# The last 512 columns of two projections in two pieces, and a first slot that multiplies high parts ahead of low parts

## The chip, the cores and the metric

The kernel runs on one core of one Trainium2 chip. The metric is the device time of one launch in microseconds (us), lower is better. TensorE does the matrix products, VectorE, ScalarE and GpSimd the rest, and SyncE issues most DMAs.

## What is computed

A decoder trunk of two layers on 256 tokens of width 1024, in float32. Cut to what matters here, a layer is

```python
x = layer_norm(alpha * x + (g_A * y_A + g_B * y_B) @ w_out, ln1_g, ln1_b)
x = layer_norm(alpha * x + (silu(conv(x @ w_up_gate)) * (x @ w_up_val)) @ w_down, ln2_g, ln2_b)
```

where y_A is a sparse attention and y_B a recurrent mix, both computed from x. The inner width of the second line is 2816. layer_norm takes the mean and the variance of the 1024 columns of each token, subtracts, scales by (var + eps)^-1/2 and applies a gain and a bias. There are four norms: A (after the out projection) and B (after the down projection) of layer 0 and of layer 1; the last one's result is the output.

## The kernel before, in words

**Split products.** The large products are float32 made of rounded parts: each weight block of 128 rows by 1024 columns lands in one of four ring slots, ScalarE copies its high part (split_hi, L1296 to L1303), VectorE subtracts to get the low part (splits_up_to, L1893 to L1902), and TensorE multiplies high by high, high by low and low by high (product, L737 to L742). Every engine runs its own list of instructions in the order in which it is written, and waits on semaphores where it needs another engine.

**Out and down projections** (token_major, L1197 to L1220). The result has the tokens on the partitions, two halves t of 128 tokens, and 1024 columns. It is held in four PSUM banks, 2 to 5, each one quarter (t, j): 128 tokens by 512 columns. For all weight blocks but the last four, each block does all four quarters. The last four blocks (the tail) are walked quarter by quarter: both quarters of t = 0, then quarter (1, 0), then quarter (1, 1). So the quarters become ready one after the other, the last with the last product. The out projection has 8 blocks, the down projection 22.

**The norm** (layer_norm, L1911 to L1992), on VectorE: added(k) adds quarter k to x in x_tok and takes its statistics with bn_stats; moments(t) merges them and adds epsilon; GpSimd raises to the power -1/2 (norm_rsqrt, L642 to L646); centered(t) subtracts the mean and multiplies by the gain; diagonal(t) makes a diagonal matrix of the scales. The written order is added 0, added 1, moments 0, centered 0, added 2, diagonal 0, added 3, moments 1, centered 1, diagonal 1. In the very last norm a first half of the output scaling ("n0a") stands in the place of diagonal 0, ahead of added 3, and no diagonal is made.

**Turning x.** TensorE multiplies x_tok by the diagonal (turned_half, L762 to L782), which scales and transposes: 16 products of 128 columns for each t, into four PSUM banks that x_banks names (L447 to L450): two pair banks (0 and 1), and 6 and 7. After norm A this is the turn "U": ScalarE evicts x's high part (xU_out, L1287), and VectorE then computes x's low part (L1980 to L1986), two column blocks at a time. After norm B of layer 0 it is the turn "T": the first products of layer 1 (L1055) stand between its two halves.

**Up projection** (split_blocks, L744 to L760). It has 22 pairs of slots, each slot 24 products of 256 columns. Slot ("up", 0) is the first. Its result goes into a pair bank, the same that holds the first two turned blocks, so every second block first waits until VectorE has made the low part of x and so has read that bank:

```python
parts = rhs(kb)
if n == ("up", 0) and b == 0 and kb % 2 == 0:
    pe.wait_ge(*dve_parts(l, f"x{kb // 2}"))
```

VectorE's order behind norm A is: diagonal 1, the low part of the first up slot's weights, the four low parts of x, the low part of the second slot's weights (L1978 to L1987), and then the rest. The slots' split high parts are made on ScalarE behind the wait for the slot that they replace.

Of the kernel before, what the change touches and what calls it, by code (L numbers as in the profile page):

```python
# [39 lines left out]
ALU = mybir.AluOpType  # L40
# [3 lines left out]
P = 128  # L44
D = 1024
T = 256
DEPTH = 2
TT = T // P
KB = D // P
# [158 lines left out]
def trunk(nc, x_in, pos_in, stream, lora_in, cpar_in, rpar_in, const_in, masks_in, out, x_dram, v_dram):  # L208
    ctx = ExitStack()
    with ctx:  # L210
        def sb(name, shape, dt=F32):
            return ctx.enter_context(nc.sbuf_tensor(name, shape, dt))
# [16 lines left out]
        def bank(n):  # L229
            return ps[:, n, :]  # L230
# [18 lines left out]
        def tok(n):  # L249

            return ps[:, n, :].rearrange("p (b t) -> p b t", t=T)
# [3 lines left out]
        x_tok = sb_or_parts("x_tok", [P, TT, D])  # L255
# [29 lines left out]
        ang = sb("ang", [P, 3, TT, NFR])  # L285
        pos = sb("pos", [P, TT], I32)
        posf = sb("posf", [P, TT])
        ln = sb("ln", [P, TT, 24])

        rs_ks, vs_dC = sb_or_parts("rs_ks", [P, 2, GB, T]), sb_or_parts("vs_dC", [P, 2, GB, T])  # L290
        tha_kkn, X_Y = sb_or_parts("tha_kkn", [P, 2, GB, T]), sb_or_parts("X_Y", [P, 2, NU, CH])
# [114 lines left out]
        slot_used = sem("slot_used")  # L406
# [14 lines left out]
        def used(l, kind, i):  # L421

            return slot_used, SLOT_AT[l, kind, i] + 1
# [21 lines left out]
        pair_at = {n: d for d, n in enumerate(pairs)}  # L445

        def x_banks(l, w):  # L447

            d = pair_at[l, ("up", 0)] if w == "U" else 0
            return d % 2, (d + 1) % 2, 6, 7  # L450

        def pair_done(l, n):
            return used(l, *pair_slots(n)[-1])
# [13 lines left out]
        def by_layer(name, steps):  # L467
            return Steps(sem(name), [steps] * DEPTH)
# [15 lines left out]
        def mids_by(gap):  # L484

            return sum(n <= gap for n in mid_last) + NM

        pe_x = by_layer("pe_x", [f"T{t}{i}" for t in range(TT) for i in range(4)] + [f"A{k}" for k in range(3)]
                        + [f"U{i}" for i in range(4)] + [f"B{k}" for k in range(3)])
        act_x = by_layer("act_x", [f"T0{i}" for i in range(4)] + ["T10", "T12"] + ["Aax"] + [f"U{i}" for i in range(4)] + ["Bax"])  # L490
        dve_par = by_layer("dve_par", ["dpar", "lsig"])
        def norm_steps(l, w):
            if l == DEPTH - 1 and w == "B":
                return ["add0", "st0", "add1", "st1", "mv0", "eps0", "c0", "add2", "st2", "n0a", "add3", "st3", "mv1", "eps1",
                        "c1", "n0", "n1a", "n1b"]
            return ["add0", "st0", "add1", "st1", "mv0", "eps0", "c0", "add2", "st2", "dg0", "add3", "st3", "mv1", "eps1",
                    "c1", "dg1", "n0", "n1a", "n1b"]

        dve_x = Steps(sem("dve_x"), [[f"mix{i}" for i in range(4)] + [w + n for w in "AB" for n in norm_steps(l, w)]
# [187 lines left out]
        def _(pe):  # L687
# [55 lines left out]

            def split_blocks(l, n, rhs):  # L744

                d = pair_at[l, n]

                def block(b, name):
                    if b == 0:
                        pe.wait_ge(*pair_free(*pairs[d - 2]))  # L750
                    w = slot_parts(l, *name)
                    for kb in range(KB):
                        parts = rhs(kb)
                        if n == ("up", 0) and b == 0 and kb % 2 == 0:
                            pe.wait_ge(*dve_parts(l, f"x{kb // 2}"))
                        mm = product(tok(d % 2)[:, b, :], [x[:, kb * P:kb * P + P] for x in w], parts,
                                     kb == 0, kb == KB - 1)
                    mm.then_inc(slot_used, 1)

                return [lambda b=b, name=name: block(b, name) for b, name in enumerate(pair_slots(n))]  # L760

            def turned_half(l, w, t):  # L762

                banks = x_banks(l, w)
                if w == "U":
                    pe.wait_ge(*dve_x(l, f"Adg{t}"))
                elif l:
                    pe.wait_ge(*dve_x(l - 1, f"Bdg{t}"))
                else:
                    pe.wait_ge(x_in_sbuf[t], 16 * (2 - t))  # L770
                for i in range(4):
                    for b in range(2):
                        dst = tok(banks[i])[:, b, t * P:t * P + P]
                        src = x_tok[:, t, (2 * i + b) * P:(2 * i + b + 1) * P]
                        if w == "T" and l == 0:
                            mm = pe.transpose(dst, src, ident)
                        else:
                            mm = pe.matmul(dst, src, diag[t], start=True, stop=True)  # L778
                    if w == "T":
                        mm.then_inc(*pe_x.inc(l, f"T{t}{i}"))  # L780
                    elif t:
                        mm.then_inc(*pe_x.inc(l, f"U{i}"))  # L782
# [261 lines left out]
            for l in L2:  # L1044
# [151 lines left out]

                def token_major(kind, n, lhs, wait, w_norm):  # L1197

                    def quarter(i, t, j):
                        w = slot_parts(l, kind, i)  # L1200
                        wait(i)
                        return product(bank(2 + 2 * t + j), [x[:, t * P:t * P + P] for x in lhs(i)],
                                       [x[:, j * 512:j * 512 + 512] for x in w], i == 0, i == n - 1)

                    tail = range(n - NS, n)
                    for i in range(n - NS):
                        for t in range(TT):
                            for j in range(2):
                                mm = quarter(i, t, j)
                        mm.then_inc(slot_used, 1)  # L1210
                    for i in tail:
                        for j in range(2):
                            mm = quarter(i, 0, j)
                            if i == n - 1:
                                mm.then_inc(*pe_x.inc(l, f"{w_norm}{j}"))
                    for i in tail:
                        mm = quarter(i, 1, 0)
                    mm.then_inc(*pe_x.inc(l, f"{w_norm}2"))
                    for i in tail:
                        quarter(i, 1, 1).then_inc(slot_used, 1)  # L1220

                token_major("out", KB, lambda i: (mix_hi[i], mix_lo[i]),
                            lambda i: pe.wait_ge(*dve_parts(l, f"mix{i // 2}")), "A")
# [414 lines left out]
        def _(dve):  # L1638
# [272 lines left out]
            def layer_norm(l, w, kind, n):  # L1911
# [1 line left out]
                s = 0.5 if w == "A" else 1.0  # L1913
                i = 2 * l + "AB".index(w)
                dve.wait_ge(*act_x(l, f"{w}ax"))
                quarter = lambda k: x_tok[:, k // 2, 512 * (k % 2):512 * (k % 2) + 512]

                def added(k):
                    dve.wait_ge(*(pe_x(l, f"{w}{k}") if k < 3 else used(l, kind, n - 1)))
                    dve.scalar_tensor_tensor(out=quarter(k), in0=bank(2 + k), scalar=s, in1=quarter(k), op0=ALU.mult,  # L1920
                                             op1=ALU.add).then_inc(*dve_x.inc(l, f"{w}add{k}"))
                    dve.wait_ge(*dve_x(l, f"{w}add{k}"))
                    dve.bn_stats(ln[:, k // 2, 6 * (k % 2):6 * (k % 2) + 6], quarter(k)).then_inc(*dve_x.inc(l, f"{w}st{k}"))

                def moments(t):
                    dve.wait_ge(*dve_x(l, f"{w}st{2 * t + 1}"))
                    dve.bn_aggr(ln[:, t, 12:14], ln[:, t, 0:12]).then_inc(*dve_x.inc(l, f"{w}mv{t}"))
# [29 lines left out]
                if l == DEPTH - 1 and w == "B":  # L1957
                    scaled(0, "n0a", 0, D // 2)
                    added(3)
                    moments(1)  # L1960
                    centered(1)
                    scaled(0, "n0", D // 2, D)
                    scaled(1, "n1a", 0, D // 2)
                    scaled(1, "n1b", D // 2, D)
                    return
                diagonal(0)
                added(3)
                moments(1)
                centered(1)
                diagonal(1)  # L1970
# [6 lines left out]
                m = KB_O + 2 * KB  # L1977
# [462 lines left out]
```

## Time and profile before

| | |
|---|---|
| median of 3 runs | 1141.61 us (1141.31 to 1144.69) |
| profiled execution | 1142.29 us |
| its span, first to last instruction | 1139.8 us |
| mean granted clock of TensorE | 0.996 of full |
| busy: TensorE / VectorE / ScalarE / GpSimd | 98% / 72% / 50% / 5% |
| matmuls | 12544 |

The span is 2.5 us shorter than the execution's own time; the rest lies around it. The profile names instructions by line, engine, operation and tiles ("ps" is PSUM, Zs and Qs hold the diagonals of t = 0 and 1, oT_r is x's low part, xT_r its high part). PE is TensorE, DVE VectorE, ACT ScalarE, POOL GpSimd. A bracket at the end of a row gives the idle time before it and what ended that.

### The profile page before, as it was taken

The numbers are of one execution on the slowest core, as the hardware profiler recorded it, in microseconds if no ns is written. First come the engines' busy times: TensorE is split into PE (matmuls) and PEld (weight loads), VectorE is DVE, ScalarE is ACT, GpSimd is POOL, SyncE is SP. The second block draws the span as 40 slices with busy tenths as digits, with TensorE's granted clock in tenths as the row PEclk, the third lists the DMA queues.
The fourth block names the chain that finished last, engine by engine and source line by source line (L and its number), as shares of the span: only waits on it lengthen the run. The fifth ranks groups of instructions, "written<-read, shape, count | busy, mean of one in ns | idle before, by whom it ended". The sixth has DMA issues, their size and how long they took to land.

```text
span 1139.8 us, 29793 instructions
## 1 busy us (share of the span) xinstructions
PE 1112.4 (98%) x12544; PEld 1013.9 (89%) x12544; DVE 815.5 (72%) x1483; ACT 567.9 (50%) x984; POOL 54.8 (5%) x49
## 2 busy tenths in 40 slices
PE   7999999999999999999999999999999999999996
PEld 7978889888898899998898888888988988999985
DVE  2678777768576887784557886868785778777745
ACT  3653555545454465563246445555463545555531
POOL 0000000000000100000010000000000000000000
PEclk9999999999999999999999999999999999999998
DMA  7433131322375456556464322222223745555651
GB/s 278 163 111 117 62 104 64 98 76 86 123 248 185 155 196 187 187 186 204 155 224 133 127 86 89 74 92 82 80 76 136 254 148 203 188 190 190 205 190 56
DMA packets 45516, 165.44 MB, mean 145 GB/s; under 512 B 5168, under 2 KB 5424, under 8 KB 45136
## 3 DMA queue, kind: packets, MB, share of 16 engines
q1 hardware_dynamic: 42736, 154.03, 40.9%
q0 software_dynamic: 1504, 7.47, 2.1%
q8 instruction: 100, 1.64, 0.6%
q10 hardware_dynamic: 1152, 2.10, 0.6%
q14 instruction: 24, 0.20, 0.1%
HBM read 160.44 MB, written 3.15 MB: 144 GB/s over the span
## 4 chain that ended last, share of the span: by engine, by line
PE 85%; DVE 10%; ACT 2%; POOL 1%; issue 1%; DMA 1%; DVEq 0%; SPq 0%; ACTq 0%
PE ps L740 22%; PE ps L741 20%; PE ps L742 19%; PE ps L897 10%; PE ps L1055 3%; PE ps L715 2%; PE ps L1109 1%; POOL g L678 1%; DVE ring_r L1653 1%; PE ps L1125 1%; DMA ring<-stream_dram 1%; PE ps L857 1%; PE ps L838 1%; PE ps L778 1%; PE ps L909 1%
## 5 line engine op out<-in xcount | busy, mean ns | idle before, releaser
L740 PE MATMUL ps<-x_tok_r,mid_hi 128*128 128x256 f32 x576 | 175.7, 305 | 0.5 <-DVE ring_r L1653 0.5
L742 PE MATMUL ps<-x_tok_r,ring_r 128*128 128x256 f32 x576 | 162.2, 282 | 0.0
L741 PE MATMUL ps<-yb_hi,mid_hi 128*128 128x256 f32 x576 | 162.1, 281 | 0.0
L740 PEld LDWEIGHTS ps<-x_tok_r,mid_hi 128*128 128x128 f32 x576 | 108.6, 189 | 9.4 <-issue 1.4
L1653 DVE TENSOR_TENSOR ring_r<-ring,mid_hi 128x1024 fp32r<-128x1024 f32 x80 | 96.9, 1211 | 19.5 <-ACT mid_hi L1251 19.2
L1251 ACT CAST mid_hi<-ring 128x1024 fp32r<-128x1024 f32 x80 | 83.8, 1048 | 52.0 <-PE ps L742 41.9
L741 PEld LDWEIGHTS ps<-yb_hi,mid_hi 128*128 128x128 f32 x576 | 108.9, 189 | 0.7 <-issue 0.7
L742 PEld LDWEIGHTS ps<-x_tok_r,ring_r 128*128 128x128 f32 x576 | 108.9, 189 | 0.0
L1901 DVE TENSOR_TENSOR rs_ks_r<-ring,tha_kkn_r 128x1024 fp32r<-128x1024 f32 x44 | 53.9, 1224 | 20.8 <-ACT tha_kkn_r L1303 20.8
L1901 DVE TENSOR_TENSOR w_lo<-ring,w_hi 128x1024 fp32r<-128x1024 f32 x42 | 51.4, 1225 | 21.0 <-ACT w_hi L1303 20.9
L1901 DVE TENSOR_TENSOR X_Y_r<-ring,arc_r 128x1024 fp32r<-128x1024 f32 x42 | 51.3, 1221 | 20.6 <-ACT arc_r L1303 20.6
L1901 DVE TENSOR_TENSOR vs_dC_r<-ring,b_k_r 128x1024 fp32r<-128x1024 f32 x44 | 53.7, 1220 | 17.2 <-ACT b_k_r L1303 17.2
L1303 ACT CAST tha_kkn_r<-ring 128x1024 fp32r<-128x1024 f32 x44 | 46.0, 1045 | 32.8 <-PE ps L742 32.8
L1770 DVE COPY_PREDICATED X_Y<-masks,ps 128x256 f32<-128x256 uint32 x80 | 35.3, 441 | 33.8 <-PE ps L897 31.0
L1303 ACT CAST arc_r<-ring 128x1024 fp32r<-128x1024 f32 x42 | 43.8, 1044 | 29.7 <-PE ps L742 19.6
L1303 ACT CAST b_k_r<-ring 128x1024 fp32r<-128x1024 f32 x44 | 45.9, 1042 | 21.7 <-PE ps L742 19.5
L1372 ACT COPY W_bt<-ps 128x256 f32<-128x256 f32 x80 | 29.6, 373 | 51.4 <-PE ps L897 38.1
L741 PE MATMUL ps<-oT_r,tha_kkn_r 128*128 128x256 f32 x192 | 53.9, 281 | 0.0
L741 PE MATMUL ps<-oT_r,arc_r 128*128 128x256 f32 x192 | 53.7, 280 | 0.0
L741 PE MATMUL ps<-oT_r,b_k_r 128*128 128x256 f32 x192 | 53.7, 280 | 0.0
L741 PE MATMUL ps<-oT_r,w_hi 128*128 128x256 f32 x192 | 53.7, 280 | 0.0
L897 PE MATMUL ps<-X_Y,nT_rb 64*64 64x64 f32 x1280 | 51.8, 222 | 1.2 <-issue 0.4
(477 smaller groups left out, 3382.8 us busy)
## 6 DMA issues: line engine op xcount, KB each, us to landing
ring<-stream_dram SPq DMA_DIRECT2D x281, 512.0 KB, 3.4
lora_w<-lora_dram POOLq DMA_DIRECT2D x2, 1536.0 KB, 7.0
W_bt<-rpar_dram POOLq DMA_DIRECT2D x4, 512.0 KB, 4.9
kt_V<-rpar_dram POOLq DMA_DIRECT2D x4, 512.0 KB, 7.4
x_tok<-x_dram SPq DMA_DIRECT2D x2, 512.0 KB, 4.1
v_saved_dram<-vs_dC ACTq DMA_DIRECT2D x4, 256.0 KB, 3.9
x_tok<-x_dram SPq DMA_DIRECT2D x1, 1024.0 KB, 5.0
vf<-v_saved_dram ACTq DMA_DIRECT2D x4, 256.0 KB, 3.3
```

Source lines behind the costliest of these rows:

```text
L715: mm = pe.matmul(dst[:, b, :], w[:, kb * P:kb * P + P], rhs[:, kb, :], start=(kb == 0), stop=(kb == KB - 1))
L740: pe.matmul(dst, lh, rh, start=start, stop=False)
L741: pe.matmul(dst, lh, rl, start=False, stop=False)
L742: return pe.matmul(dst, ll, rh, start=False, stop=stop)
L897: mm = pe.matmul(dst[q], left[q, u, :], right[q], start=start, stop=stop)
L1055: mm = pe.matmul(dst, xT[:, kb, t * P:t * P + P], w[:, kb * P:kb * P + n], start=(kb == 0), stop=(kb == KB - 1))
L1251: act.copy(mid_hi[m % NM][:, :], ring[:, n % RING, :]).then_inc(*act_mid.inc(l, m))
L1303: act.copy(w_hi[m % NS], ring[:, n % RING, :]).then_inc(*act_split.inc(l, m))
L1372: act.copy(W[:, 4 * k:4 * k + 4, :], half64("W", k)).then_inc(*act_wkv.inc(r, f"W{lev}{k}"))
L1653: dve.tensor_tensor(rounded["ring"][:, k, :], ring[:, k, :], f32(mid_hi[m % NM][:, :]), ALU.subtract).then_inc(*dve_mid.inc(l, m))
L1770: dve.copy_predicated(dst[:, 4 * k:4 * k + 4, :], mask_of(which, lev, 4), half64("XW", k)).then_inc(*dve_wkv.inc(r, name))
L1901: dve.tensor_tensor(w_lo[m % NS], ring[:, n % RING, :], f32(w_hi[m % NS]), ALU.subtract).then_inc(*dve_split.inc(l, m))
```

## The change

The tail of both projections has five pieces instead of four: (1, 1) is cut into columns 512 to 767 and 768 to 1023, in banks 5 and 6. Blocks ahead of the tail do these five pieces too. The norm adds and takes statistics of five pieces; the statistics of piece 2 are taken in two halves (st2a and st2), so that all four groups of t = 1 count 256 columns each. The turned blocks go to banks 2, 3, 7, 4 (U) and 0, 1, 7, 4 (T), with a wait for added(2) before the last pair. In slot ("up", 0) both products with x's high part run for all eight blocks first, as ScalarE delivers them, and then the eight products with the low part.

```diff
-        ln = sb("ln", [P, TT, 24])
+        ln = sb("ln", [P, TT, 48])
...
-            d = pair_at[l, ("up", 0)] if w == "U" else 0
-            return d % 2, (d + 1) % 2, 6, 7
+            return (2, 3, 7, 4) if w == "U" else (0, 1, 7, 4)
...
+                    if n == ("up", 0) and b == 0:
+                        for kb in range(KB):
+                            if kb % 2 == 0:
+                                pe.wait_ge(*act_x(l, f"U{kb // 2}"))
+                            for x in w:
+                                pe.matmul(tok(d % 2)[:, b, :], x[:, kb * P:kb * P + P], rhs(kb)[0], start=(kb == 0 and x is w[0]),
+                                          stop=False)
+                        for kb in range(KB):
+                            if kb % 2 == 0:
+                                pe.wait_ge(*dve_parts(l, f"x{kb // 2}"))
+                            mm = pe.matmul(tok(d % 2)[:, b, :], w[0][:, kb * P:kb * P + P], rhs(kb)[1], start=False,
+                                           stop=(kb == KB - 1))
...
+                    if i == 3 and t == 0 and (l or w == "U"):
+                        pe.wait_ge(*(dve_x(l, "Aadd2") if w == "U" else dve_x(l - 1, "Badd2")))
...
+                    blocks_of = [(0, 2, 0, 512), (0, 3, 512, D), (1, 4, 0, 512), (1, 5, 512, 768), (1, 6, 768, D)]
...
+                        for k in range(5):
+                            mm = part(i, k)
...
+                    for k in (2, 3):
+                        for i in tail:
+                            mm = part(i, k)
+                        mm.then_inc(*pe_x.inc(l, f"{w_norm}{k}"))
                     for i in tail:
-                        mm = quarter(i, 1, 0)
-                    mm.then_inc(*pe_x.inc(l, f"{w_norm}2"))
-                    for i in tail:
-                        quarter(i, 1, 1).then_inc(slot_used, 1)
+                        part(i, 4).then_inc(slot_used, 1)
...
+                    if k == 2:
+                        stats(k, "st2a", 0, 256)
+                        stats(k, "st2", 256, 512)
+                    else:
+                        stats(k, f"st{k}", a, b)
...
                     scaled(0, "n0a", 0, D // 2)
                     added(3)
+                    added(4)
...
                 diagonal(0)
                 added(3)
+                added(4)
                 moments(1)
```

## Rows read from the trace of the kernel before

**Rows 1.** The page, busy time by engine: us, share of the span, instructions.

```profile
PE 1112.4 (98%) x12544; PEld 1013.9 (89%) x12544; DVE 815.5 (72%) x1483; ACT 567.9 (50%) x984; POOL 54.8 (5%) x49
```

**Rows 2.** Waits of TensorE: us in total, times, longest.

```profile
PE ps L778 <- DVE Qs L1940: 4.2, 2, 2.1
```

**Rows 3.** Timeline, VectorE, norm A of layer 1: start us, us, what.

```profile
937.88 0.69 DVE L1923 BATCH_NORM_STATS2 ln<-x_tok 128x6 f32<-128x512 f32 x1
938.49 0.27 DVE L1940 TENSOR_SCALAR Zs<-const,ln 128x128 f32<-128x128 f32 x1
939.08 0.69 DVE L1920 SCALAR_TENSOR_TENSOR x_tok<-ps,x_tok 128x512 f32<-128x512 f32 x1 [0.33 <-PE ps L742]
939.81 0.69 DVE L1923 BATCH_NORM_STATS2 ln<-x_tok 128x6 f32<-128x512 f32 x1
940.53 0.21 DVE L1927 BATCH_NORM_AGGREGATE ln<-ln 128x2 f32<-128x12 f32 x1
...
942.60 0.29 DVE L1940 TENSOR_SCALAR Qs<-const,ln 128x128 f32<-128x128 f32 x1 [0.45 <-POOL ln L645]
...
944.57 3.23 DVE L1983 SCALAR_TENSOR_TENSOR oT_r<-ps,cpar,xT_r 128x256 fp32r<-128x256 f32 x8 [0.54 <-ACT xT_r L1292]
947.71 1.22 DVE L1901 TENSOR_TENSOR vs_dC_r<-ring,b_k_r 128x1024 fp32r<-128x1024 f32 x1
```

**Rows 4.** Timeline, TensorE, the same stretch.

```profile
938.65 0.40 PE L742 MATMUL ps<-arc_r,gates_r 128*128 128x512 f32 x1
...
942.95 2.05 PE L778 MATMUL ps<-Qs,x_tok 128*128 128x128 f32 x16 [2.08 <-DVE Qs L1940]
945.59 0.36 PE L740 MATMUL ps<-xT_r,tha_kkn_r 128*128 128x256 f32 x1 [0.59 <-DVE oT_r L1983]
...
948.98 0.38 PE L740 MATMUL ps<-xT_r,b_k_r 128*128 128x256 f32 x1 [0.16 <-DVE vs_dC_r L1901]
```

**Rows 5.** Timeline, TensorE, second up slot to last down product, and layer 1's first.

```profile
384.91 0.30 PE L740 MATMUL ps<-xT_r,b_k_r 128*128 128x256 f32 x1
...
506.54 0.39 PE L740 MATMUL ps<-tha_kkn_r,yb_hi 128*128 128x512 f32 x1
...
567.90 0.40 PE L742 MATMUL ps<-b_k_r,yb_r 128*128 128x512 f32 x1
...
1069.49 0.39 PE L740 MATMUL ps<-tha_kkn_r,yb_hi 128*128 128x512 f32 x1
```

**Rows 6.** Instructions of L2057 and L2336: duration in ns, min/median/max.

```profile
L2057 DVE BATCH_NORM_STATS2 ln<-p_tok x4: 209/216/222, 31.6 to 591.3; 128x6 f32<-128x64 f32 x4
...
L2336 DVE SCALAR_TENSOR_TENSOR dA<-dA,ps x22: 420/422/424, 392.0 to 1067.2; 128x256 f32<-128x256 f32 x22
```

**Rows 7.** Timeline, ScalarE, norm A of layer 1.

```profile
939.88 1.04 ACT L1303 CAST arc_r<-ring 128x1024 fp32r<-128x1024 f32 x1
943.69 3.04 ACT L1292 ACTIVATE xT_r<-ps,cpar 128x256 fp32r<-128x256 f32 x8 [2.77 <-PE ps L778]
```

**Rows 8.** Timeline, VectorE, norm A of layer 0.

```profile
378.27 0.29 DVE L1940 TENSOR_SCALAR Qs<-const,ln 128x128 f32<-128x128 f32 x1 [0.45 <-POOL ln L645]
```

**Rows 9.** Stretch of layer 0: length, TensorE's busy time, clock, DMA share, GB/s.

```profile
379.38:382.67 3.29, 3.29 (x17) 0.50 0.53 157
```

**Rows 10.** Timeline, VectorE and then TensorE, norm B of layer 0.

```profile
571.85 0.29 DVE L1940 TENSOR_SCALAR Qs<-const,ln 128x128 f32<-128x128 f32 x1 [0.44 <-POOL ln L645]
...
573.52 1.95 PE L778 MATMUL ps<-Qs,x_tok 128*128 128x128 f32 x16
```

**Rows 11.** Timeline, VectorE, the last norm.

```profile
1130.06 0.69 DVE L1923 BATCH_NORM_STATS2 ln<-x_tok 128x6 f32<-128x512 f32 x1
1130.67 0.73 DVE L1949 SCALAR_TENSOR_TENSOR x_tok<-x_tok,ln,kt_V 128x512 f32<-128x512 f32 x1
1131.32 0.68 DVE L1920 SCALAR_TENSOR_TENSOR x_tok<-ps,x_tok 128x512 f32<-128x512 f32 x1
...
1133.47 1.28 DVE L1935 SCALAR_TENSOR_TENSOR x_tok<-x_tok,ln,W_bt 128x1024 f32<-128x1024 f32 x1 [0.30 <-DVE ln L1929]
```

More of the change, by code:

```diff
@@ L486, in mids_by @@
             return sum(n <= gap for n in mid_last) + NM
-        pe_x = by_layer("pe_x", [f"T{t}{i}" for t in range(TT) for i in range(4)] + [f"A{k}" for k in range(3)]
-                        + [f"U{i}" for i in range(4)] + [f"B{k}" for k in range(3)])
+        pe_x = by_layer("pe_x", [f"T{t}{i}" for t in range(TT) for i in range(4)] + [f"A{k}" for k in range(4)]
+                        + [f"U{i}" for i in range(4)] + [f"B{k}" for k in range(4)])
         act_x = by_layer("act_x", [f"T0{i}" for i in range(4)] + ["T10", "T12"] + ["Aax"] + [f"U{i}" for i in range(4)] + ["Bax"])
@@ L493, in norm_steps @@
             if l == DEPTH - 1 and w == "B":
-                return ["add0", "st0", "add1", "st1", "mv0", "eps0", "c0", "add2", "st2", "n0a", "add3", "st3", "mv1", "eps1",
+                return ["add0", "st0", "add1", "st1", "mv0", "eps0", "c0", "add2", "st2a", "st2", "n0a", "add3", "st3", "add4", "st4", "mv1", "eps1",
                         "c1", "n0", "n1a", "n1b"]
-            return ["add0", "st0", "add1", "st1", "mv0", "eps0", "c0", "add2", "st2", "dg0", "add3", "st3", "mv1", "eps1",
+            return ["add0", "st0", "add1", "st1", "mv0", "eps0", "c0", "add2", "st2a", "st2", "dg0", "add3", "st3", "add4", "st4", "mv1", "eps1",
                     "c1", "dg1", "n0", "n1a", "n1b"]
@@ L751, in block @@
                     w = slot_parts(l, *name)
+                    if n == ("up", 0) and b == 0:
[10 more added lines that the diff above has]
+                                           stop=(kb == KB - 1))
+                        mm.then_inc(slot_used, 1)
+                        return
                     for kb in range(KB):
[L753 to L756, printed above, removed]
+                        mm = product(tok(d % 2)[:, b, :], [x[:, kb * P:kb * P + P] for x in w], rhs(kb),
                                      kb == 0, kb == KB - 1)
@@ L1197, in token_major, with part @@
                 def token_major(kind, n, lhs, wait, w_norm):
-                    def quarter(i, t, j):
+                    blocks_of = [(0, 2, 0, 512), (0, 3, 512, D), (1, 4, 0, 512), (1, 5, 512, 768), (1, 6, 768, D)]
+                    def part(i, k):
+                        t, dst, a, b = blocks_of[k]
                         w = slot_parts(l, kind, i)
                         wait(i)
-                        return product(bank(2 + 2 * t + j), [x[:, t * P:t * P + P] for x in lhs(i)],
-                                       [x[:, j * 512:j * 512 + 512] for x in w], i == 0, i == n - 1)
+                        return product(bank(dst)[:, 0:b - a], [x[:, t * P:t * P + P] for x in lhs(i)],
+                                       [x[:, a:b] for x in w], i == 0, i == n - 1)
                     tail = range(n - NS, n)
                     for i in range(n - NS):
-                        for t in range(TT):
-                            for j in range(2):
-                                mm = quarter(i, t, j)
+                        for k in range(5):
+                            mm = part(i, k)
                         mm.then_inc(slot_used, 1)
                     for i in tail:
-                        for j in range(2):
-                            mm = quarter(i, 0, j)
+                        for k in range(2):
+                            mm = part(i, k)
                             if i == n - 1:
-                                mm.then_inc(*pe_x.inc(l, f"{w_norm}{j}"))
+                                mm.then_inc(*pe_x.inc(l, f"{w_norm}{k}"))
+                    for k in (2, 3):
+                        for i in tail:
+                            mm = part(i, k)
+                        mm.then_inc(*pe_x.inc(l, f"{w_norm}{k}"))
                     for i in tail:
-                        mm = quarter(i, 1, 0)
-                    mm.then_inc(*pe_x.inc(l, f"{w_norm}2"))
-                    for i in tail:
-                        quarter(i, 1, 1).then_inc(slot_used, 1)
+                        part(i, 4).then_inc(slot_used, 1)
                 token_major("out", KB, lambda i: (mix_hi[i], mix_lo[i]),
@@ L1915, in layer_norm, with stats @@
                 dve.wait_ge(*act_x(l, f"{w}ax"))
-                quarter = lambda k: x_tok[:, k // 2, 512 * (k % 2):512 * (k % 2) + 512]
+                columns = [(0, 0, 512), (0, 512, D), (1, 0, 512), (1, 512, 768), (1, 768, D)]
+                def stats(k, name, a, b):
+                    t, m = columns[k][0], 24 + 6 * (a // (256 if columns[k][0] else 512))
+                    dve.bn_stats(ln[:, t, m:m + 6], x_tok[:, t, a:b]).then_inc(*dve_x.inc(l, f"{w}{name}"))
                 def added(k):
-                    dve.wait_ge(*(pe_x(l, f"{w}{k}") if k < 3 else used(l, kind, n - 1)))
-                    dve.scalar_tensor_tensor(out=quarter(k), in0=bank(2 + k), scalar=s, in1=quarter(k), op0=ALU.mult,
+                    t, a, b = columns[k]
+                    part = x_tok[:, t, a:b]
+                    dve.wait_ge(*(pe_x(l, f"{w}{k}") if k < 4 else used(l, kind, n - 1)))
+                    dve.scalar_tensor_tensor(out=part, in0=bank(2 + k)[:, 0:b - a], scalar=s, in1=part, op0=ALU.mult,
                                              op1=ALU.add).then_inc(*dve_x.inc(l, f"{w}add{k}"))
                     dve.wait_ge(*dve_x(l, f"{w}add{k}"))
-                    dve.bn_stats(ln[:, k // 2, 6 * (k % 2):6 * (k % 2) + 6], quarter(k)).then_inc(*dve_x.inc(l, f"{w}st{k}"))
+                    if k == 2:
[3 more added lines that the diff above has]
+                        stats(k, f"st{k}", a, b)
                 def moments(t):
-                    dve.wait_ge(*dve_x(l, f"{w}st{2 * t + 1}"))
-                    dve.bn_aggr(ln[:, t, 12:14], ln[:, t, 0:12]).then_inc(*dve_x.inc(l, f"{w}mv{t}"))
+                    dve.wait_ge(*dve_x(l, f"{w}st{4 if t else 1}"))
+                    dve.bn_aggr(ln[:, t, 12:14], ln[:, t, 24:48 if t else 36]).then_inc(*dve_x.inc(l, f"{w}mv{t}"))
                     dve.wait_ge(*dve_x(l, f"{w}mv{t}"))
```

## The prediction

> **What bounds the kernel now.** I read the page first: TensorE is busy for 98% of the span, VectorE for 72% [rows 1], so only time in which TensorE stands, or the chain behind its last product, can be won. The list of waits comes next: behind the two norms A TensorE stands 4.2 us in all, until VectorE has the second diagonal [rows 2]. What the change can win there is read from the timeline of one of them, layer 1's.
>
> The last out product starts at 938.65 and ends at 939.05 [rows 4]. VectorE adds quarter 3 at 939.08, takes statistics at 939.81, merges at 940.53, and has diagonal 1 from 942.60 [rows 3]; TensorE, done with the first turned half, stood 2.08 us and turns the second at 942.95 [rows 4]. Two things matter for the change. VectorE was idle for only 0.33 us before it added quarter 3 [rows 3]: it is nearly as late as TensorE. And behind the norm the chain runs on over VectorE: low parts of x from 944.57 for 3.23 us, then the second up slot's low weights from 947.71 to 948.93 [rows 3], and the second slot's products at 948.98 [rows 4]. The first slot's products, from 945.59, lie beside that.
>
> **TensorE's extra products.** In each layer 8 + 22 blocks turn three products of 512 columns into six of 256: 180 of 512 become 360 of 256. Start to start, products of 256 columns took (1069.49 - 948.98) / (22 x 48 - 24) = 120.51 / 1032 = 0.11677 us in layer 1's up stage [rows 4, 5]; products of 512 took (567.90 - 506.54) / (22 x 12 - 1) = 0.23331 us [rows 5]. So one pair costs 0.0002 us more, 180 of them +0.04 us. Layer 0's up stage took (506.54 - 384.91) / 1032 = 0.11786 us a product [rows 5]; at that pace it would be +0.43 us, the upper bound. A gain is excluded, the columns are the same. I take 0.04, from the undisturbed stage.
>
> The Trainium skill (TensorE: Matmul & The Clock Gate, section "Wait — 56ns, not 53.3ns?") gives each product at full clock a fixed part of about 2.5 ns beside its columns; by it the 180 additional ones would cost an estimated 0.45 us. The trace disagrees: its 512-column step is twice the 256-column one.
>
> **VectorE in norm A.** Prices first. bn_stats takes 0.694 us for 512 columns (0.69 in [rows 3]) and 0.216 for 64 [rows 6], 1.067 ns a column, so 0.42 for 256; the two rows are the bounds, and I take the line between them. An add of 256 columns with a PSUM operand takes 0.42 [rows 6]. An instruction that needs nothing of the one ahead starts 0.08 us before that one's end (0.61 after a start, for 0.69), one that does need it starts 0.04 after the end (0.73) [rows 3]. So statistics in two halves start the next instruction after 2 x 0.34 = 0.68 instead of 0.61: diagonal 0 at 938.56, and the first of the two new adds 0.19 later, at 938.75. Its piece has long been ready: the last piece is 12 products of 0.1168, 1.40 us, so piece 3 ends at about 937.65. Then come 0.46 to its statistics, 0.34 to the second add (939.55, its piece is ready at 939.05), 0.46, and 0.46 to the merge: 940.47 instead of 940.53. **Gain 0.06 us for each norm A.** The idle 0.33 and the shorter last piece are used up by two fixed parts more and by one wait more on VectorE itself. With bn_stats at 0.216, the second add would wait for TensorE (939.08), and the merge come at 939.80, a gain of 0.73; with it at 0.69 for any width, 938.49 + 0.61 + 0.19 + 0.46 + 0.61 + 0.46 + 0.73 = 941.55, a loss of 1.02. These bound it.
>
> Beside it: the wait for added(2) ahead of bank 4 has been met a microsecond earlier. The ScalarE copies for the next slots are released by piece 4, whose first block ends 9 x 0.1168 = 1.05 us before the end instead of 9 x 0.2333 = 2.10; so the last copy ends at 940.92 + 1.05 = 941.97, and the eviction behind it starts at 943.69 [rows 7]. Cost nothing; without that cover it would be 1.05. Other banks cost nothing, and a GpSimd power of one column is what it was.
>
> **High part first.** ScalarE evicts a pair of blocks in 3.04 / 4 = 0.76 us, from 943.69 [rows 7], so the pairs come at 944.45, 945.21, 945.97 and 946.73. The 16 high products start at about 944.9 and end near 947.25; the last low part is there at 944.57 + 3.23 = 947.80, and the slot is done by 948.1. The second slot's weights, however, stand behind the low parts in VectorE's list, until 948.93 [rows 3]. So TensorE starts it at 948.98 as before, and stands some 0.8 us in front of it: **gain 0** beyond the 0.06, with no loss either, for nothing is taken from VectorE.
>
> In layer 0 the clock was at half, 1.2 GHz, from 379.38 to 382.67 [rows 9]. From diagonal 1 to the second slot 384.91 - 378.27 = 6.64 us went by, against 948.98 - 942.60 = 6.38 in layer 1 [rows 3 to 5, 8]. If the fall goes away, 0.26 us come back; if it stays, TensorE has all its 24 products in a row and their order is worth nothing. I take it to stay.
>
> **Norm B of layer 0.** Diagonal 1 is ready at 572.14 and TensorE, with layer 1's first products in between, takes it at 573.52 [rows 10]. 1.38 us cover the bound of +1.02: cost nothing.
>
> **The last norm.** Here a half of the output's scaling stands before the add. VectorE went from statistics (1130.06) to scaling (1130.67) to add 3 (1131.32) with no idle time [rows 11]. Now: scaling 1130.74, add 3 1131.39, and 0.46 + 0.34 + 0.46 + 0.46 to the merge at 1133.11. Before it was 1131.32 + 1.45 (the same steps took 939.08 to 940.53 in [rows 3]) = 1132.77. **Cost 0.34 us**, uncovered: merge, centering, scaling and output all follow. Bounds as above: -0.47 (1132.30) with bn_stats at 0.216, +1.42 (1134.19) with it at 0.69. Centering also stood 0.30 us before 1133.47 [rows 11], in no other norm; that could go, and then it is a gain.
>
> **Sum.** 0.04 - 0.06 - 0.06 + 0 + 0.34 = +0.26 us on the profiled execution's 1142.29 (span 1139.8 and 2.5 around it), 1142.55. That execution was 0.68 above the median of the runs, 1141.61, so the forecast is 1141.9 us.
>
> **Rivals.** *The short pieces pay.* Statistics of 256 columns are nearly as cheap as those of 64, the half clock of layer 0 and the 0.30 us of the last norm go: 0.04 - 2 x 0.73 - 0.47 - 0.26 - 0.30 = -2.45, 1139.2 us. For it speaks that the last product's follow-up is halved; against it the line through the two bn_stats rows. Chance 0.12.
>
> *The clock falls later.* TensorE's long stand stays at 2.0 us, and 0.8 us now lie right before the second slot. In layer 0 such a stand was followed by 3.29 us at half clock [rows 9], mostly beside VectorE's chain, and so it cost 0.26. Falling on the second slot, which nothing covers, it costs half of 3.29, 1.65 us: 1143.5 in one layer, 1145.2 in both, which is slower. Layer 1 speaks against it: after the same 2.08 us its 16 turned products took 2.05 us at full clock [rows 4]. It decides as soon as the fall begins behind the turned half. Chance 0.10 for one layer, 0.03 for both. The Trainium skill (the same page, "What's actually happening") also has the gate close for an idle engine and open for a busy one; layer 0 agrees, layer 1 didn't close.
>
> *The pace of the up stage flips.* 0.11677 and 0.11786 us a product are two paces of the same code, kept through a whole stage. If layer 1 takes the slower one, 1032 x 0.0011 = +1.1, 1143.0; if layer 0 the faster, 1140.8. Chance 0.15 together.
>
> **How the numbers follow.** The forecast itself (little moves, high first gains nothing) has 0.60. What this kernel's measurement can tell from no change is about 0.3%, 3.4 us. Only the full fall of the clock in both layers is over it on the slow side (with something for what I have not seen, 0.04); on the fast side even the first rival stays inside, so 0.02; the same 0.94. The range goes from 1139.9, which leaves out the far end of the first rival, to 1143.5, which takes in one late fall and the slower pace, but not both falls.
>
> **What would show it.** The merge behind the out projection about 0.06 us earlier against the last product, with no idle time of VectorE before the fourth add; statistics of 256 columns at 0.42; a wait of some 0.8 us for the second slot's low weights, with the first slot's products starting some 0.7 us sooner after the turn; in the last norm the merge 1.9 us after the last product instead of 1.5. I am wrong if the second slot starts more than 0.3 us nearer to diagonal 1, if products of 256 between ones of 512 don't take 0.117 us, or if the granted clock falls in other places.

## The result, and the profile after

The changed kernel takes 1149.26 us in the median of 6 runs, the kernel before 1142.26 beside it: the ratio is 1.0057, with a 95% interval of 1.0045 to 1.0069. That is 7.0 us slower, clear of noise, where no change to speak of was forecast (1141.9, and 1139.9 to 1143.5 as the range). The profiled execution took 1149.79 us and spans 1147.6.

Here are the first lines of the changed kernel's page. TensorE's busy time grew by 7 us (1112.4 in [rows 1]), VectorE's by 0.9.

```profile
span 1147.6 us, 30225 instructions
## 1 busy us (share of the span) xinstructions
PE 1119.4 (98%) x12724; PEld 1030.3 (90%) x12724; DVE 816.4 (71%) x1495; ACT 567.0 (49%) x984; POOL 55.8 (5%) x49
```

So the time is not in a wait. I cut both traces at the same marks, start of a stage to start of the next (the down projection of layer 1 up to the start of the last product), in us:

| stretch | before | after | difference |
|---|---|---|---|
| up to the out projection, layer 0 | 352.15 | 352.25 | +0.10 |
| out projection, layers 0 and 1 | 22.40, 22.40 | 22.52, 22.52 | +0.24 |
| first turned half to second up slot | 10.36, 10.10 | 10.30, 10.65 | +0.49 |
| **second up slot to the down projection** | 121.63, 120.51 | 123.84, 123.93 | **+5.63** |
| down projection | 61.59, 61.36 | 61.73, 61.61 | +0.39 |
| turn after norm B, then layer 1 up to its out projection | 348.35 | 349.38 | +1.03 |
| last product's start to the end | 9.00 | 8.84 | -0.16 |

Of the 7.7 us between the spans of the two profiled executions, 5.6 lie in the up stages, in code that the change does not touch: 1032 products in each layer, one right behind the other (the only stand inside them is one of about 0.25 us at 404.4 us in layer 0 of the kernel before). Their marks on TensorE's timeline of the changed kernel, and of the norm ahead of them in layer 1, are these (start us, us, what).

```profile
946.53 3.68 PE L790 MATMUL ps<-Qs,x_tok 128*128 128x128 f32 x16 [1.97 <-DVE Qs L1966]
949.94 0.40 PE L756 MATMUL ps<-xT_r,tha_kkn_r 128*128 128x256 f32 x1
...
951.97 1.11 PE L761 MATMUL ps<-oT_r,tha_kkn_r 128*128 128x256 f32 x8
953.19 0.39 PE L739 MATMUL ps<-xT_r,b_k_r 128*128 128x256 f32 x1
...
1077.12 0.39 PE L739 MATMUL ps<-tha_kkn_r,yb_hi 128*128 128x512 f32 x1
...
1138.73 0.28 PE L741 MATMUL ps<-b_k_r,yb_r 128*128 128x256 f32 x1
```

(1077.12 - 953.19) / 1032 = 0.1201 us a product, where before it was 0.1168 [rows 4, 5]. Layer 0 has 0.1200 (0.1179 before). The same instructions, with the granted clock at full, simply start further apart. In this document the pace of a stage is this time from one product's start to the next one's.

What the change does touch went nearly as worked out. VectorE in the same norm, to be read against [rows 3]:

```profile
941.51 0.75 DVE L1936 BATCH_NORM_STATS2 ln<-x_tok 128x6 f32<-128x256 f32 x2
942.18 0.27 DVE L1966 TENSOR_SCALAR Zs<-const,ln 128x128 f32<-128x128 f32 x1
942.37 0.42 DVE L1942 SCALAR_TENSOR_TENSOR x_tok<-ps,x_tok 128x256 f32<-128x256 f32 x1
942.82 0.43 DVE L1936 BATCH_NORM_STATS2 ln<-x_tok 128x6 f32<-128x256 f32 x1
943.16 0.41 DVE L1942 SCALAR_TENSOR_TENSOR x_tok<-ps,x_tok 128x256 f32<-128x256 f32 x1
943.60 0.43 DVE L1936 BATCH_NORM_STATS2 ln<-x_tok 128x6 f32<-128x256 f32 x1
944.06 0.26 DVE L1953 BATCH_NORM_AGGREGATE ln<-ln 128x2 f32<-128x24 f32 x1
...
946.19 0.29 DVE L1966 TENSOR_SCALAR Qs<-const,ln 128x128 f32<-128x128 f32 x1 [0.45 <-POOL ln L644]
```

No idle time is left before the adds, and from the first turned half's start (938.88 before, 942.54 after) to diagonal 1 it is 3.65 us instead of 3.72.

### The profile page after: what moved, and what is told of

The parts are those of the page before. It is cut to its first block, busy times and chain, and to the rows that moved or that the text cites. A ratio compares the mean times of both kernels' runs of the same rounds, so it can differ in the third digit from the quotient of the medians.

```text
span 1147.6 us, 30225 instructions
## 1 busy us (share of the span) xinstructions
PE 1119.4 (98%) x12724; PEld 1030.3 (90%) x12724; DVE 816.4 (71%) x1495; ACT 567.0 (49%) x984; POOL 55.8 (5%) x49
## 3 DMA queue, kind: packets, MB, share of 16 engines
q8 instruction: 101, 1.65, 0.6%
## 4 chain that ended last, share of the span: by engine, by line
PE 84%; DVE 11%; ACT 1%; POOL 1%; issue 1%; DMA 1%; SPq 0%; DVEq 0%; ACTq 0%
PE ps L739 21%; PE ps L740 19%; PE ps L741 19%; PE ps L909 10%; PE ps L1067 3%; PE ps L714 2%; PE ps L1121 1%; POOL g L677 1%; DVE ring_r L1668 1%; DMA ring<-stream_dram 1%; PE ps L1137 1%; DVE ln L1936 1%; PE ps L869 1%; DVE x_tok L1942 1%; PE ps L850 1%
## 5 line engine op out<-in xcount | busy, mean ns | idle before, releaser
L1318 ACT CAST w_hi<-ring 128x1024 fp32r<-128x1024 f32 x42 | 43.7, 1041 | 17.0 <-PE ps L741 16.1
```

What stands on the lines that cost most here:

```text
L1318: act.copy(w_hi[m % NS], ring[:, n % RING, :]).then_inc(*act_split.inc(l, m))
```

## The experiments

The first question was which part of the change moves the pace of a stage that it does not touch. One line had been costed at nothing and given no term: ln grows from 24 to 48 words. All tensors made after ln then lie 192 bytes further on, and the parts of the weights are among them, while x's parts are made earlier. The stationary operand of a product is the one that a weight load (PEld, LDWEIGHTS) brings in ahead of it, the moving one is the other. The allocation in the compiled programs says where they lie (bytes within a partition):

```
            before   changed
xT, oT       41088, 73856    41088, 73856     x's parts, moving in the up stage
tha_kkn     148576   148768    high parts of the weights, stationary there
b_k         173152   173344
w_hi2       210016   210208
arc0        164960   165152
```

**e1, ln alone.** The kernel before with

```diff
-        ln = sb("ln", [P, TT, 24])
+        ln = sb("ln", [P, TT, 48])
```

> The kernel before with one line of the change: the tensor ln holds 48 words for each half instead of 24 and nothing uses the new ones, so every tile made after it lies 192 bytes further on. Theory A (the change is slow because its tiles lie elsewhere): the up stages step 0.120 us a product as in the changed kernel, and the time is 5 to 7 us above the kernel before. Theory B (the order of the first up slot sets the pace of the stage) and theory C (the mixture of 512 and 256 column pieces or the pieces' stalls set it): no change, 0 plus or minus 1 us, paces 0.1167 to 0.1178.

Measured: 1147.34 us against 1143.34, ratio 1.0037 (1.0023 to 1.0051). Both up stages have 0.1200 us a product. In layer 1:

```profile
951.25 0.28 PE L740 MATMUL ps<-xT_r,b_k_r 128*128 128x256 f32 x1
...
1075.09 0.39 PE L740 MATMUL ps<-tha_kkn_r,yb_hi 128*128 128x512 f32 x1
```

123.84 / 1032 = 0.1200. The slow pace needs none of the new instructions. The time fell short of the 5 to 7 us that were expected: it is 4.0 us longer in the median. (The ratios here are the recorded ones with their intervals; they are close to the quotients of the medians, but not the same.)

**e2, the change with the old places.**

```diff
-        ln = sb("ln", [P, TT, 48])
+        ln = sb("ln", [P, TT, 24])
...
+        lns = sb("lns", [P, TT, 24])
...
-                    dve.bn_stats(ln[:, t, m:m + 6], x_tok[:, t, a:b])
+                    dve.bn_stats(lns[:, t, m:m + 6], x_tok[:, t, a:b])
...
```

> The changed kernel, but ln keeps its 24 words and the statistics go to a small tensor of their own, made last, so that every other tile lies where it lay before. Theory A (addresses): the up stages step 0.117 to 0.118 us again and the time comes within 1 us of the kernel before (+0.3 us by the sum of the prediction). Theories B and C (order of the first slot, pieces): still 0.120 us and 6 to 7 us slower.

Measured: 1142.84 us against 1143.34, ratio 1.0002 (0.9987 to 1.0017). The up stages took 121.55 and 120.51 us, as before the change. Here are the marks of layer 1:

```profile
952.52 0.38 PE L740 MATMUL ps<-xT_r,b_k_r 128*128 128x256 f32 x1 [0.53 <-DVE vs_dC_r L1917]
...
1073.03 0.40 PE L740 MATMUL ps<-tha_kkn_r,yb_hi 128*128 128x512 f32 x1
```

This is the change as it was meant, without its side effect. The interval, 1.5 us less to 1.9 us more, holds the sum's +0.26 us but can't confirm it. Behind norm A the forecast gain is there: from the first turned half to the second up slot 10.29 and 10.01 us went by, against 10.36 and 10.10 before.

**e3, the old order of the first slot.** The changed kernel with split_blocks as it was, so with ln at 48 words.

```diff
-                    if n == ("up", 0) and b == 0:
-                        for kb in range(KB):
...
                     for kb in range(KB):
+                        if n == ("up", 0) and b == 0 and kb % 2 == 0:
+                            pe.wait_ge(*dve_parts(l, f"x{kb // 2}"))
```

> The changed kernel with the first up slot's products in the old order (each block's three products once its low part is there). Theory A (addresses): still 0.120 us a product in the up stages, 6 to 7 us slower. Theory B (order of the first slot): the up stages return to 0.117 to 0.118, and 5.6 us of the 7 are gone. Theory C (the five pieces): unchanged, 7 us slower.

Measured: 1150.01 us against 1143.34, ratio 1.0046 (1.0024 to 1.0069), up stages of 123.93 and 123.94 us. Theory B falls: the order has no part in the pace. By itself e3 can't tell theory A from C; e1 and e2 do.

**e4, high part first alone.**

```diff
-            d = pair_at[l, ("up", 0)] if w == "U" else 0
-            return d % 2, (d + 1) % 2, 6, 7
+            return (2, 3, 7, 6) if w == "U" else (0, 1, 6, 7)
```

with the changed split_blocks and the old projections.

> The kernel before with the high products of the first up slot ahead of the low ones, and the turned blocks in banks 2, 3, 7, 6; the projections keep their four quarters, ln keeps its size. Theory A (addresses): within 1 us of the kernel before, second up slot no earlier. Theory B (order of the first slot): up stages at 0.120 us, 5 to 6 us slower. Theory C: no change.

Measured: 1142.88 us against 1143.34, ratio 0.9991 (0.9978 to 1.0005). From the first turned half to the second up slot 10.37 and 10.10 us went by, against 10.36 and 10.10: high first gains nothing by itself, and TensorE waits instead. The up stages took 120.72 and 120.51 us, the old pace.

```profile
951.30 0.39 PE L739 MATMUL ps<-xT_r,b_k_r 128*128 128x256 f32 x1 [0.54 <-DVE vs_dC_r L1911]
```

So places are the cause of the slow up stages. The parts e1 and e2 together make 1.0039 of the changed kernel's 1.0057. The rest, about 2 us, is within the three intervals taken together and not explained further.

The next four ask what about the places counts. All are the kernel before with unused bytes, behind ln in e5 to e7 and ahead of the ring in e8:

```diff
+        pad = sb("pad", [P, 8])     # e5: 32 bytes; e6: 16 words, e7: 64 words
         rs_ks, vs_dC = sb_or_parts("rs_ks", [P, 2, GB, T]), sb_or_parts("vs_dC", [P, 2, GB, T])
...
+        pad = sb("pad", [P, 48])    # e8
         ring = sb_or_parts("ring", [P, RING, D])
```

**e5, 32 bytes.**

> The kernel before with 32 unused bytes after ln: the weights' parts and all later tiles lie 32 bytes further on, x's parts where they lay. In the kernel before the weights begin 96 bytes past a multiple of 128 and x's parts on one; with 192 bytes more the weights begin 32 past it. Now both are on a multiple of 128. Theory A1 (what counts is where the weights begin within 128 bytes): another pace than 0.1167 or 0.1200, and as the aligned place perhaps the fastest, 0.116 or less, up to 2 us faster. Theory A2 (what counts is how far weights and x's parts lie from each other): also another pace. Theory A3 (any shift of tiles by less than 256 bytes upsets it): 0.120, 5 us slower.

**e6, 64 bytes.**

> The same with 64 unused bytes: the weights begin 32 bytes past a multiple of 128, as in the changed kernel, but only 64 bytes from where they lay. Theory A1: 0.120 us a product in the up stages, 4 to 6 us slower than before. Theory A2: not settled by it (the distance to x's parts is 32 bytes over a multiple of 128, as in the changed kernel). Theory A4 (64 bytes are the unit, so that 96 and 32 are the same): 0.117.

**e7, 256 bytes.**

> The same with 256 unused bytes: the weights begin 96 bytes past a multiple of 128 again, as in the kernel before, but further away from the start than in the changed one. Theory A1 and theory A2: 0.1167 to 0.1178, time within 1 us of the kernel before. A theory by which a larger shift or less free memory is at fault: 0.120.

**e8, 192 bytes ahead of everything.**

> The kernel before with 192 unused bytes ahead of the ring: weights and x's parts both lie 192 bytes further on, their distance is that of the kernel before. Theory A1 (place of the weights): 0.120, 5 us slower. Theory A2 (distance between weights and x's parts): 0.1167 to 0.1178, within 1 us.

Measured, with the distance from x's parts to the weights' parts counted within 256 bytes (before: 148576 - 41088, which leaves 224):

| | distance | a product of 256 columns, up stages | down stages, us | ratio (interval) |
|---|---|---|---|---|
| before | 224 | 0.1179, 0.1168 | 61.59, 61.36 | |
| e1 | 160 | 0.1200, 0.1200 | 61.38, 61.16 | 1.0037 (1.0023 to 1.0051) |
| e5 | 0 | 0.1201, 0.1201 | 59.98, 59.64 | 1.0034 (1.0020 to 1.0047) |
| e6 | 32 | 0.1184, 0.1184 | 61.02, 60.79 | 1.0012 (1.0001 to 1.0024) |
| e7 | 224 | 0.1168, 0.1168 | 61.59, 61.37 | 1.0000 (0.9981 to 1.0018) |
| e8 | 224 | 0.1174, 0.1168 | 61.59, 61.35 | 1.0004 (0.9983 to 1.0026) |

e8 decides between A1 and A2. Its weights lie exactly where e1's lie, only x's parts are 192 bytes further on too, and the pace is back (0.1174 in layer 0 includes a short stand; outside it the products step 0.1167). e6 had spoken against A1 already: 0.1184, where A1 wanted 0.120, and A4 falls with it, which wanted 0.117. e7 rules out a larger shift or less free memory.

```profile
947.32 0.39 PE L741 MATMUL ps<-xT_r,b_k_r 128*128 128x256 f32 x1 [0.16 <-DVE vs_dC_r L1902]
...
1067.84 0.39 PE L741 MATMUL ps<-tha_kkn_r,yb_hi 128*128 128x512 f32 x1
```

120.52 us against 123.84 in e1. What counts is where the two operands lie to each other. e5 came out at the 0.120 of theory A3 (any shift below 256 bytes), not as the fastest that A1 hoped for; e6's 0.1184 shows that shifts do not all act alike. And e5 gave a surprise: its products of 512 columns come 59.64 / 263 = 0.2268 us apart instead of 0.2333.

```profile
1073.56 0.40 PE L741 MATMUL ps<-tha_kkn_r,yb_hi 128*128 128x512 f32 x1
...
1133.20 0.39 PE L743 MATMUL ps<-b_k_r,yb_r 128*128 128x512 f32 x1
```

**e9 and e10, four distances in one kernel.** The slots use four buffers for their weights' parts in turn. Both kernels are the kernel before with these tensors reordered in pairs, with padding between them:

```diff
+        pad0 = sb("pad0", [P, 8])     # e9: 32, 32, 128, 64 bytes; e10: 96, 32, 32, 64
+        rs_ks, tha_kkn = sb_or_parts("rs_ks", [P, 2, GB, T]), sb_or_parts("tha_kkn", [P, 2, GB, T])
+        pad1 = sb("pad1", [P, 8])
+        vs_dC, b_k = sb_or_parts("vs_dC", [P, 2, GB, T]), sb_or_parts("b_k", [P, 2, NU, CH])
...
```

> The kernel before with its weight parts laid out so that the four buffers, which the slots use in turn, lie at four distances from x's parts, counted within 256 bytes: 0 (tha_kkn, rs_ks), 32 (b_k, vs_dC), 160 (w_hi2, w_lo2) and 224 (arc0, X_Y). These are the four distances tried so far, one at a time: 0.120, 0.118, 0.120 and 0.1167 us a product of the up stage. If the distance within 256 bytes sets the pace product by product, each buffer shows its own pace inside this one kernel. If the pace is a state of the whole stage, or follows from something else that those kernels had, all four buffers show one pace.

> The same with the four distances not tried yet: 64 (tha_kkn, rs_ks), 96 (b_k, vs_dC), 128 (w_hi2, w_lo2) and 192 (arc0, X_Y). By the theory of the distance each buffer shows a pace of its own, between 0.1067 (256 columns at the granted 2.4 GHz) and 0.12 us. If only a multiple of 128 bytes matters, 96 runs at 0.1167 (as 224 does) and 128 at 0.120 (as 0 does). No prediction for 64 and 192 beyond that; one of them may be faster than the kernel before.

Measured: one timeline of e9 shows all four paces, one behind the other. These are the first products of five slots that follow each other in layer 1, each slot 24 products:

```profile
1041.02 0.28 PE L747 MATMUL ps<-xT_r,tha_kkn_r 128*128 128x256 f32 x1
...
1043.89 0.28 PE L747 MATMUL ps<-xT_r,b_k_r 128*128 128x256 f32 x1
...
1046.72 0.28 PE L747 MATMUL ps<-xT_r,w_hi 128*128 128x256 f32 x1
...
1049.60 0.28 PE L747 MATMUL ps<-xT_r,arc_r 128*128 128x256 f32 x1
...
1052.40 0.28 PE L747 MATMUL ps<-xT_r,tha_kkn_r 128*128 128x256 f32 x1
```

2.87, 2.83, 2.88 and 2.80 us for 24 products at distances 0, 32, 160 and 224: 0.1196, 0.1179, 0.1200 and 0.1167. The means over the last 95 us of each stage are 0.1195, 0.1182, 0.1199 and 0.1167, in both layers alike, and within 0.0006 of what whole kernels gave. The pace goes by the distance, product by product. e10 gave 0.1179 at 64, 0.1174 at 96, 0.1182 at 128 and 0.1179 at 192; so 128 bytes are not the unit (96 is not 224, and 128 not 0), and of the eight places in steps of 32 bytes 224 has the fastest pace seen. That 0.1167 is not always what 224 gives: the kernel before shows 0.1178 there in layer 0. Whether the four places of e10 have a second pace as well, its single execution can't tell. Each of these two is a single execution (1147.54 us against 1143.06, and 1142.78): their verdict rests on the paces, not on the times.

**e11 and e12, a layout of its own.** The up stage does best with 224 between stationary and moving operand; e5 says that the products of 512 columns do better with 0. Both can be had, since xT and oT are no operands of the out and down projections (besides the up stage, only products of a layer's first part read them):

```diff
-        xT = sb_or_parts("xT", [P, KB, T])
...
-        oT = sb_or_parts("oT", [P, H_A, T])
-        qT = oT
...
+        pad = sb("pad", [P, 8])
+        xT = sb_or_parts("xT", [P, KB, T])
+        oT = sb_or_parts("oT", [P, H_A, T])
+        qT = oT
         cpar = sb("cpar", [P, DEPTH, NCPAR])
```

> The kernel before with the order of its tensors changed and 32 unused bytes: x's parts for the up projection (xT, oT) lie 32 bytes past a multiple of 256 plus 128, everything else that the projections multiply lies on it. By the theory of the distance the up stages have 224 between weights and x's parts (0.1167 us a product, as the kernel before at its best), and the out and down stages 0 (0.227 us a product of 512 columns, as with 32 bytes of padding): down stages 61.4 to 59.8 us, out stages 22.4 to 21.9, up stages 120.5 each; the products with yb_hi, o_hi and the mids lose up to 1 us in all. Sum: 4.5 us less, 1 us lost, 3 to 4 us faster than the kernel before, ratio 0.997. If the two effects don't combine: no change, or 3 us slower as with the padding alone.

e12 makes the ring and mid_hi behind gates and yb as well, with 224 bytes of padding ahead of them and 64 behind.

> The same, and the ring and the two high parts of the middle weights (mid_hi) also lie 224 bytes from x's parts x_tok and yb_hi, within 256. The products of the first part of a layer (576 of each of the three lines, 0.118 to 0.119 us apart in the kernel before) then come down to 0.1167 where TensorE is what bounds them. Up to 2 us less than the layout above where they bound, about 1 us, since much of that stretch waits for VectorE: 4 to 5 us faster than the kernel before, ratio 0.996. If the distance matters only for the up stages, the same time as the layout above.

Measured: e11 takes 1139.02 us against 1142.67, **ratio 0.9972 (0.9961 to 0.9983)**, as expected: up stages of 120.40 and 120.51 us, out stages of 21.89 and 21.90, down stages of 60.00 and 59.67. Marks of layer 1, from the second up slot to the last product:

```profile
947.14 0.38 PE L741 MATMUL ps<-xT_r,b_k_r 128*128 128x256 f32 x1 [0.17 <-DVE vs_dC_r L1902]
...
1067.65 0.40 PE L741 MATMUL ps<-tha_kkn_r,yb_hi 128*128 128x512 f32 x1
...
1127.32 0.39 PE L743 MATMUL ps<-b_k_r,yb_r 128*128 128x512 f32 x1
```

e12 takes 1137.81 us, ratio 0.9964 (0.9948 to 0.9981). The intervals overlap, so what the ring and mid_hi add in time stays open. The pace of the products that it aims at (three times 576 of 256 columns, their unbroken steps) did move as expected: 0.1186 us in the kernel before, 0.1196 in e11, where they lie at distance 0, and 0.1174 in e12. Both are faster than the kernel before and the changed one.

## Why the prediction was wrong

**The step that failed** is a term that the sum put at nothing without a reason. It took the pace of all other products as given, and the doubled ln, which moves the weights' parts by 192 bytes, had no term. It costs +5.63 us in the up stages of the profiled executions (0.1200 us a product for 0.1168 and 0.1179), and e1 alone, with that one line, is 4.0 us slower in the median. With it taken back (e2) the change costs +0.02% with an interval of 0.15% to each side, which holds the sum's +0.26 us (0.02%). That agreement is partly luck: of the sum's terms the projections came out 0.20 us dearer and the last norm about 0.4 us cheaper than forecast, as told below.

The rival of the two paces had looked at the right rows and stopped too early. It took 0.11677 and 0.11786 us as states into which the same code falls by chance, priced a flip at 1.1 us and stopped there; that a product's spacing hangs on where its operands lie, with 0.120 as a third value, it did not ask. A part of it holds: at distance 224 both values appear in one and the same kernel (0.1179 and 0.1168 in the two layers of the kernel before; 121.65 us in layer 1 of e12, 120.40 in layer 0). What picks between these two is not settled. In layer 0 of the kernel before the products stepped 0.1168 before a short stand at 404.4 us and 0.1178 behind it. In e4 it went the other way at a stand at 407.1 us, from 0.1178 to 0.1168. In e8 the products step 0.1167 on both sides of a stand of half a microsecond. So it can change in the middle of a stage, which is not the "kept through a whole stage" of the prediction.

Term by term, profiled executions:

- **Products in pieces of 256**: forecast +0.04. In e2, where places are the old ones, out stages take 22.43 instead of 22.40, down stages 61.62 and 61.51 instead of 61.59 and 61.36: +0.24. The direction was right, the size too small. The prediction compared unlike products: those of 256 columns had their operands at distance 224, those of 512 at 0 and 32 in turn, so that "twice the 256-column one" held by chance and says nothing against a fixed part for each product. At one and the same distance, 0, two products of 256 take 0.240 us and one of 512 takes 0.2268 (e5): one product more costs 0.013. In a layout like e11's the same cut would cost an estimated 180 x 0.013 = 2.4 us by these values, which no run here tried. So neither 0.0002 nor the 2.5 ns that the prediction cites holds everywhere; e2's 0.24 us are 1.3 ns for each of the 180.
- **VectorE in norm A**: forecast 0.06 gained in each; 0.07 measured to diagonal 1. Statistics of 256 columns took 0.43 (0.42 forecast). The merge of 24 words takes 0.05 more than that of 12, which was left out.
- **High part first**: forecast nothing, measured nothing (e4), and the wait for the second slot's weights is the 0.54 us that e4's row shows, not the 0.8 that I gave.
- **The half clock** in layer 0 stayed, as taken. In layer 1 of the changed kernel it came as well, on the turned half, and from diagonal 1 to the second slot 953.19 - 946.19 = 7.00 us went by instead of 6.38. That resembles the rival of the late fall, but it began with the turn and not on the second slot, and cost 0.6 us instead of 1.65. It is not the change's doing: layer 1 fell to half in e1, e5, e7 and e12 as well, which have the old pieces and the old order, and not in e2 and e3, which have the new pieces. In e2, where both kernels' layer 1 ran at full clock, the stretch is 0.09 us shorter than before.

The fall in layer 1 is seen in one stretch of the changed kernel (length, then busy time of TensorE, its weight loads, VectorE, ScalarE and GpSimd, TensorE's clock, DMA share, GB/s):

```profile
946.53:949.94 3.41, 3.41 (x17) 3.41 (x17) 2.39 (x5) 2.15 (x6) 0.00 (x0) 0.51 0.34 102
```

- **Norm B of layer 0**: 5.40 us between the halves against 5.39. Covered, as said.
- **The last norm**: forecast +0.34, measured -0.04 (from the last product's end to the end of the span: 8.60 us before, 8.56 after). The merge did come 1.8 us after that end instead of 1.5, but the 0.30 us of standing before the centering [rows 11] went, the possibility that the prediction named:

```profile
1140.82 0.26 DVE L1953 BATCH_NORM_AGGREGATE ln<-ln 128x2 f32<-128x24 f32 x1
1141.12 0.15 DVE L1955 TENSOR_SCALAR ln<-ln 128x1 f32<-128x1 f32 x1
1141.21 1.28 DVE L1961 SCALAR_TENSOR_TENSOR x_tok<-x_tok,ln,W_bt 128x1024 f32<-128x1024 f32 x1
```

It went in e2 and e3 too, which have five pieces, and stayed (0.30 to 0.31) in all ten kernels of the experiments that keep four quarters. So it goes with the pieces. By what was not tried.

The +1.03 us from the turn of layer 0 through the first part of layer 1 belongs to no term: over all the kernels here that stretch took between 348.1 and 349.6 us (349.1 in e4, whose places are those of before), and single executions of the kernel before spread from 1139 to 1147 us. Its cause was not looked for; I take it for scatter.

## What to carry to other kernels

Making a tensor longer moves every tensor behind it, and that is an edit of its own: on a kernel whose time is TensorE's, compare the spacing of products in a stage that the edit does not touch, and if it moved, make the new words a tensor of their own behind all others, as e2 did. The spacing can be worth setting on purpose: here 32 bytes of padding and two tensors made later gave 3.6 us of 1142.7. Of the layouts tried the best was not the same for both widths, distance 224 for 256 columns and 0 for 512, so it has to be measured for the products at hand. And a shorter last piece helps only where the engine behind it was waiting for it; VectorE had 0.33 us to spare, and fixed costs took that.

## What the runs showed of the hardware

- The spacing of float32 products in rounded parts, at full granted clock and without any wait, hangs on the distance in bytes between stationary and moving operand within a partition. For 256 columns: 0.1195 to 0.1201 us at 0, 0.1182 to 0.1184 at 32, 0.1179 at 64, 0.1174 at 96, 0.1182 at 128, 0.1199 to 0.1201 at 160, 0.1179 at 192, 0.1167 or 0.1178 at 224 (64, 96, 128 and 192 from one execution, e10). A shift of 256 bytes changes nothing (e7). For 512 columns with every operand at distance 0 it is 0.2268 (e5, e11), and 0.2333 in the kernel before, where the stationary operands lie at 0 and 32 in turn.
- What in the chip does that is not shown. The overlap of a product with the next one's weight load is a guess, which fits that both operands' places matter. The Trainium skill (TensorE: Matmul & The Clock Gate, section "Step-by-step: what each phase is for") says that loading the next weights takes no SBUF bandwidth from the running product; by that alone places should not matter, and the runs show that they do.
- Behind norm A TensorE stood 1.9 to 2.1 us in each layer of every kernel here, and what the granted clock did then differs from one profiled execution to another: it fell to half in layer 0 alone (before, e2, e3, e4, e9, e10, e11), in layer 1 alone (e5), in both (the changed kernel, e1, e7, e12) or in neither (e6, e8). e7 and e8 differ from the kernel before in unused bytes alone. Where it fell, the way from the first turned half to the second up slot took some 0.3 to 0.6 us longer (10.72 and 10.75 us in e7, 10.11 and 10.10 in e8).
